# Reordering the first loads of a decoder layer: which queue issues the eight tiles of x, and when

## The reference, cut to what matters

```python
xn = rmsnorm(x, g1)
z = xn @ w_in
q, k, v, o, ig, fg, u, vb, ga, gb = split_in(z)
...
x = x + (jax.nn.sigmoid(ga) * y_a + jax.nn.sigmoid(gb) * y_b) @ w_o
xn = rmsnorm(x, g2)
up = xn @ w_up
...
x = x + (jax.nn.silu(a) * gval) @ w_down
```

## Time and profile before

| what | value |
|---|---|
| median of 3 runs | 909.52 us (909.24, 909.52, 912.8) |
| the profiled execution's own time | 908.81 us |
| its span, first to last instruction | 907.1 us |
| TensorE busy | 899.0 us (99%) |
| VectorE, ScalarE, GpSimd busy | 525.6, 364.6, 134.0 us |
| DMA, mean over the span | 111 GB/s, 100.24 MB |

### The profile page before, as it was taken

The page is one execution under the profiler, slowest core; times in us unless marked ns, Lnnn a source line. Parts: engine busy times, 40 slices in busy tenths (PEclk is TensorE's granted clock), DMA queues, the critical chain, the costliest instruction groups (busy, mean ns, idle before and its releaser), DMA issues.

```text
span 907.1 us, 19519 instructions
## 1 busy us (share of the span) xinstructions
PE 899.0 (99%) x7402; PEld 894.8 (99%) x7402; DVE 525.6 (58%) x817; ACT 364.6 (40%) x560; POOL 134.0 (15%) x181
## 2 busy tenths in 40 slices
PE   9999999999999999999999999999999999999997
PEld 8999999999999999999999999999999999999997
DVE  7895875444884444433336777777777777433234
ACT  7545335535862323322223344444444444322232
POOL 0672000011541111000016500000000000000001
PEclk9999999999999999999999999999999999999998
DMA  6332262243962222522334222222222222323322
GB/s 211 124 110 94 71 229 74 71 138 123 326 232 80 83 71 69 179 100 92 92 113 101 80 84 92 92 92 92 92 92 92 92 92 87 99 85 93 98 85 95
DMA packets 31341, 100.24 MB, mean 111 GB/s; under 512 B 4652, under 2 KB 7244, under 8 KB 31048
## 3 DMA queue, kind: packets, MB, share of 16 engines
q1 hardware_dynamic: 29256, 92.96, 30.9%
q0 software_dynamic: 1328, 5.72, 2.3%
q10 hardware_dynamic: 720, 1.04, 0.3%
HBM read 92.37 MB, written 7.35 MB: 110 GB/s over the span
## 4 chain that ended last, share of the span: by engine, by line
PE 91%; issue 3%; POOLq 3%; DMA 1%; POOL 1%; DVEq 0%; ACT 0%; DVE 0%; SPq 0%; ACTq 0%
PE out L1450 86%; PE trp L1450 2%; POOLq L1428 2%; PE aux L1450 1%; POOLq L1426 1%; PE trp L1482 1%; DMA raw_pair<-in_w_slots 0%; PE aux L1639 0%; DMA cwb<-in_conv_wb 0%; POOL y L1441 0%; POOL out_conv_old L1412 0%; DVEq L1269 0%; ACT whi L475 0%; POOLq L1419 0%; DVE wlo L840 0%
## 5 line engine op out<-in xcount | busy, mean ns | idle before, releaser
L840 DVE TENSOR_TENSOR wlo<-raw_pair,whi 128x1024 fp32r<-128x1024 f32 (+1 forms) x145 | 186.3, 1285 | 211.8 <-ACT whi L475 211.5
L475 ACT ACTIVATE whi<-raw_pair 128x1024 fp32r<-128x1024 f32 (+2 forms) x152 | 155.4, 1024 | 268.6 <-PE out L1450 264.8
L1450 PE MATMUL out<-xh,whi 128*128 128x260 f32 x768 | 158.7, 288 | 0.0
L1450 PE MATMUL out<-xh,wlo 128*128 128x260 f32 x768 | 154.6, 283 | 0.0
L1450 PE MATMUL out<-xl,whi 128*128 128x260 f32 x768 | 154.3, 282 | 0.0
L1450 PE MATMUL out<-x2h,wlo 128*128 128x260 f32 x704 | 141.9, 283 | 0.0
L1450 PE MATMUL out<-x2h,whi 128*128 128x260 f32 x704 | 141.8, 282 | 0.0
L1450 PE MATMUL out<-x2l,whi 128*128 128x260 f32 x704 | 141.6, 283 | 0.0
L1450 PEld LDWEIGHTS out<-xh,whi 128*128 128x128 f32 x768 | 118.7, 189 | 0.5
L1450 PEld LDWEIGHTS out<-xh,wlo 128*128 128x128 f32 x768 | 118.3, 188 | 0.0
L1450 PEld LDWEIGHTS out<-xl,whi 128*128 128x128 f32 x768 | 118.2, 188 | 0.0
(11 more groups left out here) (283 smaller groups left out, 1378.4 us busy)
## 6 DMA issues: line engine op xcount, KB each, us to landing
raw_pair<-in_w_slots SPq DMA_DIRECT2D x123, 512.0 KB, 3.3
raw_pair<-in_w_dn SPq DMA_DIRECT2D x16, 448.0 KB, 3.4
c_ring<-in_C_state SPq DMA_DIRECT2D x8, 512.0 KB, 5.5
row<-scratch SPq DMA_DIRECT2D x8, 512.0 KB, 5.8
out_C_sample<-c_ring SPq DMA_DIRECT2D x8, 512.0 KB, 4.7
raw_pair<-in_w_dn SPq DMA_DIRECT2D x8, 512.0 KB, 3.5
xres<-in_x_all POOLq DMA_DIRECT2D x1, 2080.0 KB, 11.0
x<-in_x_all SPq DMA_DIRECT2D x5, 260.0 KB, 6.4
```

Of the source, the lines that this page charges most:

```text
L475: return act.activation(out, in_, func, **kw_)
L840: TT(wlo[p][:, 0:width], raw[p][:, 0:width], whi[p][:, 0:width].bitcast(F32), ALU.subtract)\
L1450: return pe.matmul(*a, **k)
```

## The change

Tiles 1, 2 and 4 of x change their issuer or their place. At its start ScalarE issues tile 0 alone. It issues tile 2 right behind its rounding of tile 0, and tile 4 right behind its rounding of tile 1. SP takes tile 1, between `first_load(0)` and `first_load(1)`, and no longer issues tile 4. The number of transfers and their sizes are the same.

```diff
@@ block.sync
             sp.dma_start(gains[:, :, :], ins["gains"]).then_inc(s_g, 16)
             first_load(0)
+            load_x(1)
             first_load(1)
             load_x(3)
-            load_x(4)
             for t in range(2):
@@ block.scalar
-            for k in range(3):
+            def act_load_x(k):
+
                 act.dma_start(x0[:, k, :], ins["x_all"][:, k, :]).then_inc(s_x[k], 16)
+
+            act_load_x(0)
             act.wait_ge(s_init, 1)
             table_of_sqrt()
...
             for k in range(KT):
                 act.wait_ge(s_x[k], 16)
                 A(xuh[:, k, :], x0[:, k, :], scale=gains[:, 0, k:k + 1]).then_inc(s_xuh, 1)
+                if k < 2:
+                    act_load_x(2 + 2 * k)
                 if k in (0, 2, 4):
```

## The result

The changed kernel takes 911.25 us (median of 20 runs, 910.78 to 913.16), the kernel before 909.32 us (median of 20, 908.69 to 912.8). The ratio is 1.0024, 95% interval 1.0017 to 1.003: 1.9 us slower, resolved although it is under half a per cent. (A ratio given here is worked out over all runs of the two kernels and can differ in the last digits from the quotient of the medians, here 1.0021.) The forecast was 0.4 us less. The span of the profiled execution went from 907.1 to 909.1 us.

What follows compares the result with a forecast made beforehand. Arrivals in the head were taken to pace an otherwise unbroken matmul queue: TensorE begins 0.4 us earlier, tile 2 permits 0.45, tile 4 costs nothing, so the median goes from 909.52 to 909.1 us, range 908.0 to 911.0.

Steps and rivals of the forecast that it cites:

- What bounds the kernel, and how a shift travels: Head, unbroken matmul queue, tail: a gain in the head comes off the end in full if nothing behind becomes late.
- two arrivals: In the head: the first weight piece and x tile 2 set the pace, and a gain needs both earlier.
- The first weight piece: Head, queue q1: without tile 1 beside it, lands 0.5 us earlier, at about 4.84 us; its rounding starts at 4.86.
- The ceiling of the text: Head, TensorE: warm-up matmuls end at 5.24 us, so products cannot begin before; gain at most 0.68 us.
- rival 2: Head, TensorE: the warm-up, lasting up to 6.5 us, sets the start; no gain, 909.5 us; chance 0.12.
- Issues on ScalarE: Head: tile 2's issue costs 0 to 0.2 us, half charged; TensorE begins at 5.52 us, 0.4 us earlier.
- Tile 2: Head, q10: issued at about 4.2 us, lands 3.1 us later at 7.3 us, 0.45 us earlier than before.
- Tile 4: Head: issued at about 5.7 us, lands at 8.8 to 9.5; cost 0 to 0.25 us, most likely 0.
- Rival 3: Head: late tiles 2 and 4 meet the old backlog, tile 2 taking 6.0 us; 911.9 us, worst 914; chance 0.05.
- Rival 1: Head: SP's full queue holds up tile 2, landing at 8.0 to 8.2 us; no gain, up to 910.0 us; chance 0.25.
- SP's slow issue of tile 5: Head, at 4.23 us: took 0.88 us where others take 0.47, cited as a sign that something was full.

Runs made afterwards that it cites:

- e3_x1_moved: Against the changed kernel: ScalarE issues tiles 0 and 2 at its start, SP issues tile 4 behind tile 3, only tile 1 stays moved; 909.04 us, ratio 1.0.
- e5_needed_order: The order of need, against the changed kernel: ScalarE issues only tile 0, SP all else, tile 2 behind tile 1, tile 4 behind tile 3; 909.11 us, ratio 0.9996.
- e9_late_on_sp: Against the changed kernel: SP issues the late tiles too, tile 2 between the two later weight pieces, tile 4 behind tile 7; 911.65 us, ratio 1.0027.
- e7_sp_holds: Against the changed kernel: tile 2 stays late, SP waits for the rounding of tile 0 before issuing tiles 3, 4 and all behind; 909.44 us, ratio 1.0001.
- e8_order_warm8: Same as e5_needed_order, with eight warm-up matmuls in place of ten; 908.81 us, ratio 0.9995 to the kernel before.
- e2_x2_late: Against the changed kernel: tile 4 goes back to SP behind tile 3, tile 2 alone stays late; 911.05 us, ratio 1.002.
- e1_x4_late: Against the changed kernel: tile 2 goes back to ScalarE's start, tile 4 alone stays late behind the rounding of tile 1; 911.1 us, ratio 1.0019.
- e4_probes: Against the kernel before: three extra 16 KB loads issued by ScalarE, at 2.26, 3.73 and 18.29 us; 909.4 us, ratio 1.0002.
- e11_before_warm8: Against the kernel before: eight warm-up matmuls in place of ten, nothing else; 910.59 us, ratio 1.0012.

## Why the prediction was wrong

**What bounds the kernel, and how a shift travels: right.** Arrivals pace the head, and what the head has lost at k = 5 is lost at the end: k = 5 is 1.97 us later, the span 2.0, the time 1.9. A shift of the start alone does not travel so: `e3_x1_moved` began 0.41 us later and lost nothing, `e5_needed_order` began 0.43 us earlier and won nothing. The text counted two arrivals; in the changed kernel tile 4 was a third.

**The first weight piece: the direction right, the closeness in part luck.** Forecast landing 4.84 us, measured 1.27 + 3.5 = 4.77. Where q10 held nothing beside the weight piece its rounding began at 4.34 to 4.85 us (`e9_late_on_sp`, `e7_sp_holds`, `e8_order_warm8`, the changed kernel, `e2_x2_late`, `e5_needed_order`), where it held a tile at 5.36 to 5.89. The saving is real, and its size varies by half a microsecond. First product forecast at 5.52 us, measured 5.49; that is luck too. The rounding at 4.76 us would have allowed 5.32. The end of the warm-up held it: with ten warm-up matmuls the first product began at 5.45 to 5.49 us in five kernels, whether that rounding was at 4.34 or at 4.85, and with eight at 5.00. The ceiling of the text, 5.24 us, lay too early, since the warm-up did not speed up this time. The window from 4.6 to 5.2 us, the kernel before first, then the changed one:

```profile
4.35 0.88 PE L1450 MATMUL aux<-ones 128*128 128x128 f32 x6
4.35 1.06 PE L1454 MATMUL aux<-ones 128*128 128x128 f32 x4
```

That is rival 2, in a smaller size. Its 0.265 us a pass counted overlapping passes as if they stood in a row: twenty slow passes ended at 5.49 us, (5.49 - 1.20) / 20 = 0.21 us each, and not at 6.5.

**Issues on ScalarE: the lower bound was right.** Both issues ran beside the rounding ahead of them (3.71 beside 3.70, 5.94 beside 5.93) and cost nothing. Half of 0.2 us had been charged. The two issues that left the start did free something: in the kernel before, the dummy Sqrt ran from 3.56 to 3.76 us, past tile 0's landing, and without them tile 0 was rounded at 3.70 instead of 3.86. So tile 2 was issued at 3.71 us, before the forecast 3.9 to 4.6, and that should have helped it.

**Tile 2: the step that failed.** The text took 3.1 us to landing, between the bounds 2.9 and 3.9, from rows in which the backlog was counted in the tile's own queue: "It is nearest to the first, since q10 has nothing ahead of it". It took 5.7 us. In this head a transfer's packets wait for what the other engine has issued before it as well: `e1_x4_late` (q10 empty, not a packet for 3.2 us while q1 moved 1.2 MB), `e7_sp_holds` (SP holds back, first packet after 1.4 us, landing after 4.6) and `e9_late_on_sp` (same place, other queue, 5.2 us) show it; `e4_probes` (16 KB, 5.7 us) agrees. The earlier trace rows could not have told it. The second weight piece, issued by SP at 1.74 us, took 5.8 us, and tile 2, issued by ScalarE at 1.76 us, took 6.0. That fits the order of issue, but counting in the own queue does not exclude it: at the 0.23 and 0.13 MB per us of the earlier trace rows, the three tiles of q10 (0.80 MB) take 3.5 us and the two pieces of q1 (0.52 MB) 4.0, an estimate that leaves them alike too. The rows left both readings open, and the forecast stood on one. The price that it quoted beside this from the Trainium skill (DMA: Bandwidth & Descriptors, Anatomy of one DMA — SWDGE (gpsimd) path), 2.6 us for a tile of x, is given there for transfers that GpSimd issues, and was further off than its own 3.1.

**Tile 4: the same mistake.** Forecast 3.1 us to landing and a cost of 0 to 0.25 us, "most likely 0"; measured 5.9. Behind the late tile 2 it added 0.27 us between k = 2 and k = 5 (1.97 against 1.70), but it is what the last chain runs over, and `e1_x4_late` shows that it costs 2 us without tile 2's help. Both terms had to be right for the forecast to hold.

**The rivals.** Rival 3 had the mechanism and the size: landing after 6.0 us, 911.9 us; measured 5.7 and 911.25. It was given 0.05, on the argument that those 6.0 us were spent behind two tiles in the same queue. That argument was the untested part of the whole forecast, and it deserved no such weight. The rival itself names no cause for a backlog, only that it stays. Rival 1 had the right suspicion, that SP's full queue holds up ScalarE's tile, but priced it as one delayed issue, 8.0 to 8.2 us; the issue was not delayed (0.36 us long), the packets were, by 3.0 us. Whether SP's slow issue of tile 5 was a sign of the same thing was not tested. The chance of 0.97 for under 0.5% held: 0.24% is inside. The upper end of the range, 911.0 us, did not reach to the rival's 911.9.

## What to carry to other kernels

Count the line before a transfer over all issuers, not in its own queue: here a load issued "just in time" behind a list of prefetches of another engine took 5.5 to 6.5 us, where 2.9 had been seen for the first tile. If a load must be issued late, hold the other engine's issues back too, or issue it early in the place where it is needed. And check the next arrivals before counting on an earlier start: here 0.43 us won at the first product were lost again by k = 5 even in the order of need.

## What the hardware showed unexpectedly

- **One line for two queues.** A transfer in an empty queue had no packet moved for 3.0 us after its issue (3.2 us in `e1_x4_late`), while the other queue worked off its list; with that list held back it was 1.4 us. The Trainium skill (DMA: Bandwidth & Descriptors, Queues, rings and completion order) says that SP and ScalarE each own a row of rings but no descriptor generator of their own. A common generator that works in order of issue would give what the runs show; that this is where the line stands was not shown.
- **A lower rate from 3.75 to 5.5 us where only one queue was open.** The mean rate in that stretch, before, changed, `e2_x2_late`, `e9_late_on_sp` in this order (last number; the columns ahead are the busy times of TensorE, its weight loads, VectorE, ScalarE and GpSimd, granted clock, share of the DMA engines):

```profile
3.75:5.50 1.75, 1.49 (x10) 1.29 (x9) 0.76 (x1) 0.87 (x3) 0.00 (x0) 1.00 0.98 329
```

```profile
3.75:5.50 1.75, 1.75 (x11) 1.75 (x10) 0.96 (x2) 1.40 (x3) 0.00 (x0) 1.00 0.86 249
```

```profile
3.75:5.50 1.75, 1.75 (x11) 1.75 (x10) 0.95 (x2) 1.40 (x3) 0.00 (x0) 1.00 0.85 211
```

```profile
3.75:5.50 1.75, 1.75 (x11) 1.75 (x10) 0.95 (x2) 1.31 (x3) 0.00 (x0) 1.00 0.89 206
```

  All seven kernels with tile 1 or tiles 2 to 4 in q10 by then had 303 to 354 GB/s, the six in which q1 worked alone for most of the stretch 206 to 296. The text had said that the bytes per us do not change with the queues. At 80 GB/s less for 1.75 us, 0.14 MB or some 0.4 us of transfers fell behind in the changed kernel. Why was not tested. One open queue is not by itself slower: in `e1_x4_late` q1 alone gave 385 GB/s from 5.5 to 6.5 us, with 265 of 332 packets under 2 KB, and from 9 to 11 us it gave 402 GB/s and more in several of these kernels.
- **An issue overtakes the ACTIVATE ahead of it** by up to 0.45 us (3.73 against 4.18), and it runs beside a table load.
- **The same transfer varies from kernel to kernel**: in three kernels with the same issues up to there (before, `e4_probes`, `e11_before_warm8`) the rounding of the first weight piece began at 5.36, 5.44 and 5.89 us. The head's numbers from one execution are good to about half a microsecond.
